# Expert stage of a hybrid layer: half of the down projection's output columns in three short-format passes, its operands split by ScalarE and VectorE

## The reference

```
xs = x_pad[slot_tok].reshape(n_blk, MOE_BLOCK, D)            # blocks of 128 slots, D = 1024
def expert_block(args):
    xb, e = args
    return (jax.nn.silu(xb @ w_gate[e]) * (xb @ w_up[e])) @ w_down[e]   # 1024 -> 256 -> 1024
out = zeros.at[slot_tok].add(ys * slot_w[:, None])
```

## Time and profile before

| | |
|---|---|
| median of three runs | 1693.89 us |
| the profiled execution's own time | 1691.28 us |
| its span | 1689.5 us |
| mean granted TensorE clock | 0.938 of full speed |
| PE, DVE, ACT busy over the span | 87%, 62%, 38% |
| expert stage, first gather to last scatter | 1294.8 to 1636.5 us of the span |
| PE, DVE, ACT busy in one steady turn of 10.05 us | 10.05, 7.81, 6.25 us |
| DMA share in the expert stage | 0.9 to 1.0 of the 16 DMA engines |

### The profile page before, as it was taken

One profiled execution on the slowest core, in us unless ns is written; L12 is line 12 of the kernel. 1 busy time (PEld: TensorE's weight loads), 2 busy tenths in 40 slices (PEclk: granted clock), 3 DMA queues, 4 the chain that ended last, 5 costly groups with the idle time before them and its releaser, 6 DMA issues. The chain is left out here.

```text
span 1689.5 us, 21107 instructions
## 1 busy us (share of the span) xinstructions
PE 1465.5 (87%) x7063; PEld 1075.4 (64%) x7079; DVE 1043.4 (62%) x2037; ACT 636.9 (38%) x1115; POOL 398.3 (24%) x404
## 2 busy tenths in 40 slices
PE   6995999999999878998598889989973999999960
PEld 3464788898885547777366664438972677777740
DVE  4168999999803546666477661223335777777736
ACT  3167111122112136656366661001111666566622
POOL 1002212222201034431344411220002133333313
PEclk9997899999999989999799999999985999999985
DMA  7450132322330000000643204222226799999807
GB/s 191 51 92 1 62 97 96 100 72 92 98 106 1 1 1 1 1 1 1 201 101 89 64 1 174 75 66 76 75 108 268 271 358 352 356 371 376 344 31 310
DMA packets 83435, 216.80 MB, mean 128 GB/s; under 512 B 23624, under 2 KB 42600, under 8 KB 71064
## 3 DMA queue, kind: packets, MB, share of 16 engines
q1 hardware_dynamic: 72984, 194.72, 34.8%
q0 software_dynamic: 9216, 16.80, 2.7%
q10 hardware_dynamic: 1152, 4.19, 0.6%
HBM read 187.75 MB, written 44.70 MB: 138 GB/s over the span
## 5 line engine op out<-in xcount | busy, mean ns | idle before, releaser
L457 DVE TENSOR_SCALAR_CACHE_REDUCE mask<-score,cand 128x272 bf16<-128x272 f32 (+6 forms) x224 | 185.5, 892 | 5.0 <-DVE cand L476 4.9
L2039 DVE TENSOR_TENSOR w_rest<-wgu,w_lead 128x1024 fp32r<-128x1024 f32 x128 | 155.9, 1222 | 45.0 <-ACT w_lead L1986 43.8
L1100 DVE TENSOR_TENSOR pL<-ps,pH 128x512 fp32r<-128x512 f32 (+3 forms) x224 | 126.9, 574 | 85.0 <-ACT pH L1044 82.1
L542 PE MATMUL ps<-hHi,g_lead 128*128 128x512 f32 (+2 forms) x416 | 159.0, 382 | 16.2 <-DVE hLo L582 16.2
L543 PE MATMUL ps<-hLo,g_lead 128*128 128x512 f32 (+2 forms) x416 | 159.0, 382 | 0.0
L544 PE MATMUL ps<-hHi,g_rest 128*128 128x512 f32 (+2 forms) x416 | 158.2, 380 | 0.0
L1044 ACT CAST pH<-ps 128x512 fp32r<-128x512 f32 (+3 forms) x224 | 108.3, 492 | 120.0 <-PE ps L989 119.9
L1986 ACT CAST w_lead<-wgu 128x1024 fp32r<-128x1024 f32 x128 | 134.4, 1055 | 37.8 <-PE ps L1932 37.8
L1930 PE MATMUL ps<-w_lead,x_lead 128*128 128x512 f32 x256 | 113.9, 445 | 6.0 <-DVE w_rest L2039 6.0
L1952 PE MATMUL ps<-wd,hmT 128*128 128x512 f32 x256 | 115.3, 593 | 1.6 <-DVE hmT L2062 1.0
L577 POOL TENSOR_TENSOR g_rest<-g_raw,g_lead 128x2048 fp32r<-128x2048 f32 x13 | 61.7, 4745 | 228.5 <-ACT g_lead L551 228.5
(11 more groups left out here) (323 smaller groups left out, 3402.3 us busy)
## 6 DMA issues: line engine op xcount, KB each, us to landing
wgu<-in_w_exp_gate SPq DMA_DIRECT2D x32, 1024.0 KB
wgu<-in_w_exp_up SPq DMA_DIRECT2D x32, 1024.0 KB
wd<-in_w_exp_down SPq DMA_DIRECT2D x32, 1024.0 KB, 13.8
g_raw<-in_w_in SPq DMA_DIRECT2D x14, 1024.0 KB, 5.9
gates_d<-stage SPq DMA_DIRECT2D x32, 256.0 KB, 2.0
gt<-gates_d SPq DMA_DIRECT2D x32, 256.0 KB, 3.1
rel_d<-relf SPq DMA_DIRECT2D x1, 4672.0 KB
KR<-kb_d SPq DMA_DIRECT2D x16, 260.0 KB, 6.4
```

What stands on the lines that cost most here:

```text
L457: return dve.tensor_scalar(mask[:, OFF[i]:OFF[i + 1]], score[:, OFF[i]:OFF[i + 1]], thr, 0.0, op, ALU.add, accum_out=cnt[:, i:i + 1])
L542: pe.matmul(dst, x[0], y[0], start=(k == 0), stop=False)
L1100: dve.tensor_tensor(pL[n % RING][:, lo:512], bank_of(k)[:, lo:512], pH[n % RING][:, lo:512].bitcast(F32), ALU.subtract).then_inc(s_rs, 1)
L2039: dve.tensor_tensor(w_rest[u][:, :, 2 * part:2 * part + 2, :], wgu[u][:, :, 2 * part:2 * part + 2, :], w_lead[part][:, :, :, :].bitcast(F3 ...
```

## The change

The first 512 output columns of the down projection are done in three short-format passes; the other 512 stay in float32 and now go first. Each turn gets four new instructions on the other engines:

- ScalarE, at the head of the turn: `down_lead(n)` copies `wd[:, :, 0:512]` to `d_lead` (128 x 1024 elements). `d_lead` has one buffer, so it waits for `down(n-1)`. Before the sigmoid: `hidden_lead(n)` copies the transposed hidden values to `hT_lead` (128 x 256).
- VectorE, at the head of the turn: `down_rest(n)` subtracts `d_lead` from `wd` in place. In `mid(n)`: the copy to `hmT` now also waits for `hT_lead` (`m_hl`), and after it stands the subtraction that gives `hT_rest` (128 x 256).
- PE: `down(n)` has two float32 matmuls in the program (four in the trace) where it had four (eight), and six short-format ones behind them, which wait for `d_rest` and `hT_rest`.

The core of the diff:

```
+            for k in range(2):
+                pe.matmul(ps[:, 6, :], hmT[u % 2][:, k, :], wd[u][:, k, HD2:D], start=(k == 0), stop=(k == 1))
+            pe.wait_ge(S["m_dr"], n + 1)
+            pe.wait_ge(S["m_hr"], n + 1)
+            for k in range(2):
+                pe.matmul(ps[:, 5, :], hT_lead[u % 2][:, k, :], d_lead[:, k, :], start=(k == 0), stop=False)
+                pe.matmul(ps[:, 5, :], hT_lead[u % 2][:, k, :], d_rest[u][:, k, 0:HD2], start=False, stop=False)
+                mm = pe.matmul(ps[:, 5, :], hT_rest[u % 2][:, k, :], d_lead[:, k, :], start=False, stop=(k == 1))
...
+            def down_lead(n, turn_n, u, first):
+                act.wait_ge(WD[u], turn_n * 16 + 16)
+                if not first:
+                    act.wait_ge(S["m_y"], n)
+                act.copy(d_lead[:, :, :], wd[u][:, :, 0:HD2]).then_inc(S["m_dl"], 1)
+
+            def hidden_lead(n, u, first):
+                act.wait_ge(S["m_th"], n + 1)
+                if not first:
+                    act.wait_ge(S["m_y"], n - 1)
+                act.copy(hT_lead[u % 2][:, :, :], ps[:, 4, 0:2 * P].rearrange("p (k n) -> p k n", k=2)
+                         ).then_inc(S["m_hl"], 1)
...
+                dve.wait_ge(S["m_hl"], n + 1)
                 dve.tensor_copy(hmT[u % 2][:, :, :], ps[:, 4, 0:2 * P].rearrange("p (k n) -> p k n", k=2)
                                 ).then_inc(S["m_ht"], 1)
+                dve.tensor_tensor(hT_rest[u % 2][:, :, :], ps[:, 4, 0:2 * P].rearrange("p (k n) -> p k n", k=2),
+                                  hT_lead[u % 2][:, :, :].bitcast(F32), ALU.subtract).then_inc(S["m_hr"], 1)
...
+            def down_rest(n, u):
+                dve.wait_ge(S["m_dl"], n + 1)
+                dve.tensor_tensor(d_rest[u][:, :, 0:HD2], wd[u][:, :, 0:HD2], d_lead[:, :, :].bitcast(F32),
+                                  ALU.subtract).then_inc(S["m_dr"], 1)
...
             def turn(n, u, half, first, ahead=True):
+                down_rest(n, u)
...
             turn(NE - 2, 2, NE // 2 - 1, False, False)
+            down_rest(NE - 1, U - 1)
             mid(NE - 1, 1, False)
```

More of the change, by code:

```diff
@@ L173, in hybrid_layer @@
         top = keep("top", 2)
+        R_OT = small[0]
         otok = [keep(f"otok{k}", 4 * P) for k in range(2)]
@@ L1535, in hybrid_layer @@
         experts(nc, a, at, sem, block, ps, flat, con, h1, nhalf, tabs, xn2_d, ys_d, out, R_H, R_K, ss, var, rstd,
-                wts)
+                wts, R_OT)
 U = 4
@@ L1823, in experts @@
 def experts(nc, a, at, sem, block, ps, flat, con, h1, nhalf, tabs, xn2_d, ys_d, out, R_H, R_K, ss, var, rstd,
-            wts):
+            wts, R_OT):
     tok_i, dst_i, slot_w, ov_e = tabs["tok_i"], tabs["dst_i"], tabs["slot_w"], tabs["ov_e"]
@@ L1839, in experts @@
     w_lead = [at(f"w_lead{k}", [P, 2, 2, FE], F32R, wts["end"] + 16384 + 4096 * k) for k in range(4)]
+    HD2 = D // 2
+    d_lead = at("d_lead", [P, 2, HD2], F32R, R_OT)
+    d_rest = [at(f"d_rest{u}", [P, 2, D], F32R, R_K + 24576 * u + 16384) for u in range(U)]
+    hT_lead = [at(f"hT_lead{k}", [P, 2, P], F32R, R_H + 30720 + 1024 * k) for k in range(2)]
+    hT_rest = [at(f"hT_rest{k}", [P, 2, P], F32R, wts["end"] + 32768 + 1024 * k) for k in range(2)]
     w_rest = [at(f"w_rest{u}", [P, 2, KT, FE], F32R, R_K + 24576 * u) for u in range(U)]
     ident = con[:, K_ID:K_ID + P]
-    names = ["m_tk", "m_tx", "m_xa", "m_xd", "m_gp", "m_wl", "m_wr", "m_sg", "m_h1", "m_h2", "m_th", "m_ht",
+    names = ["m_tk", "m_tx", "m_xa", "m_xd", "m_gp", "m_wl", "m_wr", "m_dl", "m_dr", "m_hl", "m_hr", "m_sg", "m_h1", "m_h2", "m_th", "m_ht",
              "m_y", "m_ya", "m_yd", "m_st", "m_dk", "m_xz", "m_wk", "m_ask"]
@@ L1938, in hidden_T @@
                 pe.wait_ge(S["m_ht"], n)
+                pe.wait_ge(S["m_hr"], n)
             for k in range(2):
@@ L2008, in result @@
                                scale=wk[u % 2][:, 0:1]).then_inc(S["m_ya"], 1)
+            def down_lead(n, turn_n, u, first):
[9 more added lines that the diff above has]
+                         ).then_inc(S["m_hl"], 1)
             def turn(n, r, u, half, first, early, ahead=True):
+                down_lead(n, r, u, early)
                 if ahead:
@@ L2013, in turn @@
                         lead(n + 2, r + (u + 2) // U, (u + 2) % U, part, False)
+                hidden_lead(n, u, first)
                 back(n + 1, u + 1, False)
@@ L2027, in _ @@
             for n in range(2):
-                turn(n, 0, n, 0, True, True)
+                turn(n, 0, n, 0, True, n == 0)
             with act.Fori(0, (NE - 4) // 4) as r:
@@ L2031, in _ @@
                     turn(r * 4 + (u + 2), r + (u + 2) // U, (u + 2) % U, r * 2 + (1 + u // 2), False, False)
-            turn(NE - 2, 0, 0, NE // 2 - 1, False, False, False)
+            turn(NE - 2, NE // U - 1, U - 2, NE // 2 - 1, False, False, False)
+            down_lead(NE - 1, NE // U - 1, U - 1, False)
+            hidden_lead(NE - 1, U - 1, False)
             result(NE - 1, NE // 2 - 1, 1, False)
@@ L2098, in _ @@
                 if n == 0:
+                    down_rest(0, 0)
                     for part in range(2):
```

## The result

The changed kernel takes 1697.68 us (median of 20 runs, 1693.03 to 1704.80); the kernel before, in the same comparison, 1692.64 us (20 runs, 1684.46 to 1699.32). The ratio is 1.0034 with a 95% interval of 1.0019 to 1.0049: slower by 5.7 us (3.2 to 8.3). The forecast was +1.6 us, with most of the chance (0.59) on a time within 0.2% of before. The time lies in the range of 1689 to 1702 us, but the kernel is slower, by 0.34%, and the interval excludes no change. (In one later run, the other last turn alone, one execution of twelve took 3782 us, where the rest took 1690.7 to 1701.8; the ratio leaves it out.)

A forecast was written before the change was run, and what follows sets the result against it. PE, busy for all of each 10.05 us turn, was taken as the bound. Per turn -0.35 of work and +0.34 of wait gave -0.3 us over 30 turns, plus 1.9 at the end: +1.6, or 1695.5 us, range 1689 to 1702.

The forecast's parts named there:

- PE's work, -0.35 us a turn: Steady turn: four float32 matmuls (1.72 us) give way to six short-format ones (1.37), leaving PE 9.70 us of work.
- The hand-over, +0.34: Steady turn: hmT waits for hT_lead, so PE waits 0.34 us before down, including 0.02 for slower hops.
- the bounds 0.24 to 0.50: Limits on PE's wait per steady turn: quick copy without restart cost, or both hand-overs at 0.12; -3 to +4.5 us overall.
- What lies beside it: Steady turn: d_lead, d_rest and hT_rest stay hidden beside PE; VectorE rises to about 9.3 us, x_rest's cover 0.0 to 0.3.
- The end of the stage, +1.9 us: Turns 30 and 31: the longer chain adds 0.06 us, then 1.87 with d_rest ahead of hmT.
- VectorE's chain to `x_rest`: Rival: gate_up also waits for x_rest in steady turns; 1700 us, up to 1705; chance 0.24.
- The clock: Rival: PE's clock falls in the steady turns' new holes, +23 us, to 1718; chance 0.04.
- The wait doesn't bind: Rival: hT_lead comes early enough that PE's saving arrives in the turns; -8.6 us, to 1685.3; chance 0.06.
- DMA holds the turn: Rival: transfers keep the turn at 10.05 us, taking up to 10.5 us of gain; no chance of its own.
- Part of the wait: Rival: PE waits only 0.10 to 0.24 us a turn; 1688.3 to 1692.5 us; chance 0.09.

The follow-up runs named there:

- the other last turn alone: Changed kernel; in the last turn only, hT_lead goes ahead of d_lead, hmT and hT_rest ahead of d_rest: 1696.58 us, ratio 1.0009.
- the hand-over alone: Kernel before plus ScalarE's hT_lead (not read) and hmT waiting for it; down stays eight float32 matmuls: 1707.04 us, ratio 1.0092.
- the splits alone: Kernel before plus d_lead and d_rest, split values unused, PE waiting for d_rest half way through a float32 down: 1698.11 us, ratio 1.0037.
- fewer waits: Changed kernel without implied waits: hmT waits for hT_lead alone, hT_lead for the transposes alone: 1696.34 us, ratio 1.0023.
- the other source: Changed kernel with hmT copied straight from the transposes, hT_lead then made from hmT behind the sigmoid, hT_rest later: 1684.70 us, ratio 0.9962.
- the other last turn: Last turn with hmT ahead of d_rest, in two kernels: the changed one (1696.58 us) and the one making hT_lead from hmT (1682.26 us).

## Why the prediction fell short, step by step

**PE's work, -0.35 us a turn: right.** The period without any wait is 9.701 us, where the prediction had 9.70.

**The hand-over, +0.34: the step that failed, by its size.** The mechanism is as forecast: the hand-over alone costs 0.45 us a turn, and 10.145 - 9.701 = 0.44 in the changed kernel, and the gain is spent in it. The chain was worked out with 0.04 us from `hT_lead` to `hmT`; it is 0.13 in the changed kernel, and 0.04 once the implied waits are gone, which brings the turn to the forecast 10.04. A hop of 0.12 was at hand and was taken as the exception, with 0.02 us for it; where the copy itself has the last wait it is the exception, one turn in four, but the new hop from ScalarE has its wait in the instruction ahead in every turn. 0.45 lies inside the bounds 0.24 to 0.50, near the edge whose end the prediction gave as +4.5 us over the turns. (The lower bound doesn't come out of its own terms: 0.34 less 0.065 for the quick copy and 0.07 for the restart is 0.20.) The turns bring 30 x 0.091 = +2.7 us instead of -0.3.

**What lies beside it: right.** `d_lead` and `d_rest` cost the steady turn nothing (10.052 in the run with them alone). VectorE is busy for 9.1 us a turn where 9.3 were forecast.

**The end of the stage, +1.9 us: right at full clock, short by the clock.** `hmT` ends 3.25 us after the end of `down(30)` (1634.66 - 1631.41), 3.33 forecast; the last turn is 1.82 us longer, 1.87 forecast; from the last steady turn on it is +2.09 in all. Not foreseen was what such a hole does to the clock. Five profiled executions have the 3.12 us: this kernel's two, and those of the splits alone, of fewer waits and of the other source. In four of them PE was then granted about half clock for most of the last group, at +1.6 to +1.7 us; in one it kept 1.00. Behind the shorter holes it kept 1.00 each time: 1.00 us before, 0.99 and 1.42 with the other last turn, 1.42 with the hand-over alone. If four in five holds for the runs that were timed, that is an estimate of 0.8 x 1.6 = +1.3 us on their mean.

The trace of before had the warning at the head of the stage, and the prediction didn't read it. PE, at a clock of 1.00 from 1309.00 to 1312.00, is idle for 3.02 us, and then works at half clock, with steps of 0.43 us in the short format (two rows, and the window):

```profile
1315.80 0.77 PE L1930 MATMUL ps<-w_lead,x_lead 128*128 128x512 f32 x1 [3.02 <-DVE w_rest L2039]
1316.36 0.63 PE L1931 MATMUL ps<-w_rest,x_lead 128*128 128x512 f32 x1
```

```profile
1315.80:1318.50 2.70, 2.70 (x7) 2.12 (x8) 2.70 (x3) 2.68 (x3) 0.00 (x0) 0.50 0.97 410
```

All nine profiled executions have this hole of 3.02 us, and in all nine the clock is at half at most 0.3 us after PE starts again.

Sum: 2.7 + 2.1 + 1.3 = 6.1 us against the measured 5.7 (3.2 to 8.3). What the forecast lacked is some 0.1 us in one hop, times 30, and the clock of one turn. That the time still lies in the range is in part luck: its upper part was there for VectorE's chain, which didn't bind.

**The rivals.** *VectorE's chain to `x_rest`* had most of the chance for slower, and it isn't what made the kernel slower: there is no idle time of PE ahead of gate and up, neither at 10.15 us a turn nor at 9.70, where VectorE has 0.5 us left. *The clock* was weighed for the wrong holes. The steady turns' holes of 0.17 to 0.22 us left it at 1.00 all the way from 1350 to 1600 us. So the rule of the Trainium skill, "TensorE: Matmul & The Clock Gate", section "A second HAM failure mode: psum-queue depth-cycling", on a PE that idles briefly between groups, wasn't seen to act here. The clock fell after one long hole, which the prediction itself had computed (2.22 us more) and priced as idle time alone. *The wait doesn't bind*: it did here, and with the other source of `hT_lead` it doesn't, which gives what that case had for the turns. *DMA holds the turn*: not at 9.70 us, with a share of 1.00 and 407 GB/s in the turn shown; from 1350 to 1600 us the waits of that trace name no DMA. *Part of the wait* is out: the wait was more than forecast, not less.

**What stays open.** What puts the last wait into an instruction ahead or into the copy: no run changes that alone, with all three waits kept. How often the clock falls in the last turn of runs without a profile: 4 of 5 is all there is. And some 2.5 us in the ratio of the run with the splits alone, which no row of the stage accounts for. Executions differ by as much ahead of the stage's turns: the first transposes of `hm` come at 1322.24 and 1319.65 us in the two profiles of the changed kernel.

## What to carry to other kernels

Where one engine is full and the hand-over to it fits with less than 0.1 us to spare, a step put into that hand-over costs nearly its whole length in every turn; price the chain hop by hop, and if a new value can be made from the old hand-over's result instead of ahead of it, make it there. An instruction that waits for something implied by another of its waits can pay for it at each turn, when the wait that ends last lands in an extra instruction ahead of it, so wait for the last event alone. And look at the last turn of a loop by itself: it has no neighbour's work to cover a reordered step, and a long idle time there may cost clock beside its own length.

## What the runs showed of the hardware

- The hop from one engine's end to `hmT` or `hT_lead` was 0.03 or 0.04 us where the copy itself waited for the semaphore that came last (all 25 turns with fewer waits, 19 of 25 before), and 0.10 to 0.14 where an instruction ahead of it did: 0.035 to the start of that instruction, 0.021 or 0.050 in it, 0.044 behind it, for the hop from ScalarE. With the hand-over alone, one turn of each four was slower still at `hT_lead`, 0.19 to 0.40.
- After 3.12 us without a matmul the clock fell to half in four of five executions (0.53 and 0.59 in the windows shown), at the same idle time to the hundredth; after the 3.02 us at the head of the stage in nine of nine; after the 1.42, 0.99 or 1.00 us of the last turn in none of four.
- The core's loads ran at 407 GB/s with a share of 1.00 for a turn of 9.70 us (371 GB/s over 1350 to 1600 us of that run), and nothing waited for them.
